# Seven block products in place of eight, and the order of the work behind two norms

## The reference

```
x = x + merged @ w_out                       # 512x1024 by 1024x1024
hn = rms_norm(x, ffn_norm)
up = causal_depthwise_conv(hn @ w_up, ffn_conv_w)
gate, val = split(up, 2)
x = x + (silu(gate) * val) @ w_down          # 512x2816 by 2816x1024
x = rms_norm(x, final_norm)
h = x @ w_in_2                               # first product of the second block
```

## Time and profile before

| what | us |
|---|---|
| runs | 1055.69, 1053.08, 1054.73 |
| median | 1054.73 |
| span of the profiled execution | 1050.5 |
| PE busy in it | 1038.4 |
| DVE, ACT, POOL busy | 593.9, 445.9, 51.0 |
| w_out, first matmul to the first transposes | 274.4 to 315.2 |
| norm 1 and `first_three` | 315.2 to 341.2 |
| first half of w_down begins | 444.7 |
| norm 2, first transposes | 681.0 |

### The profile page before, as it was taken

The page is one execution under the profiler, slowest core; times in us unless marked ns, Lnnn a source line. Parts: engine busy times, 40 slices in busy tenths (PEclk is TensorE's granted clock), DMA queues, the critical chain, the costliest instruction groups (busy, mean ns, idle before and its releaser), DMA issues.

```text
span 1050.5 us, 13952 instructions
## 1 busy us (share of the span) xinstructions
PE 1038.4 (99%) x5453; PEld 846.1 (81%) x5453; DVE 593.9 (57%) x1110; ACT 445.9 (42%) x855; POOL 51.0 (5%) x71
## 2 busy tenths in 40 slices
PE   9999999999999999999999999999999999999997
PEld 7877778888888888888888888899888677777785
DVE  6466665445356666533466563553456673567757
ACT  5355542233345434431234442453244454556640
POOL 0000000000001100000000000125200001000000
PEclk9999999999999999999999999999999999999999
DMA  7421133222341842333122323334211222511012
GB/s 277 160 65 57 61 101 100 95 89 98 123 140 41 275 152 87 98 125 110 61 101 85 100 97 110 131 122 135 91 61 61 61 81 71 211 41 41 21 61 80
DMA packets 29106, 107.08 MB, mean 102 GB/s; under 512 B 3227, under 2 KB 3371, under 8 KB 28401
## 3 DMA queue, kind: packets, MB, share of 16 engines
q1 hardware_dynamic: 24864, 86.13, 24.8%
q0 software_dynamic: 4032, 19.96, 5.3%
q10 hardware_dynamic: 144, 0.10, 0.0%
HBM read 101.44 MB, written 7.36 MB: 104 GB/s over the span
## 4 chain that ended last, share of the span: by engine, by line
PE 88%; DVE 5%; ACT 4%; issue 2%; DMA 2%; DVEq 0%; SPq 0%; ACTq 0%
PE ps L780 26%; PE ps L782 25%; PE ps L781 25%; PE ps L1054 2%; PE ps L1222 2%; PE ps L1205 1%; PE ps L1187 1%; DMA raw<-wp 1%; ACT whi L1285 1%; PE ps L1143 1%; PE ps L1106 1%; ACT SC L1336 1%; PE ps L1175 1%; DVE wlo L1633 0%; DVE SC L1739 0%
## 5 line engine op out<-in xcount | busy, mean ns | idle before, releaser
L780 PE MATMUL ps<-XH,whi 128*128 128x512 f32 (+1 forms) x864 | 336.7, 390 | 0.6 <-DVE XL L1646 0.2
L782 PE MATMUL ps<-XH,wlo 128*128 128x512 f32 (+1 forms) x864 | 326.9, 378 | 0.0
L781 PE MATMUL ps<-XL,whi 128*128 128x512 f32 (+1 forms) x864 | 326.5, 378 | 0.0
L1633 DVE TENSOR_TENSOR wlo<-raw,whi 128x1024 fp32r<-128x1024 f32 (+1 forms) x158 | 191.6, 1218 | 166.7 <-ACT whi L1285 166.1
L1285 ACT CAST whi<-raw 128x1024 fp32r<-128x1024 f32 (+1 forms) x158 | 161.2, 1027 | 95.9 <-PE ps L782 70.5
L780 PEld LDWEIGHTS ps<-XH,whi 128*128 128x128 f32 x864 | 162.6, 188 | 43.0 <-issue 12.4
L782 PEld LDWEIGHTS ps<-XH,wlo 128*128 128x128 f32 x864 | 162.6, 188 | 31.2
L781 PEld LDWEIGHTS ps<-XL,whi 128*128 128x128 f32 x864 | 162.8, 188 | 27.8 <-issue 0.5
L780 PE MATMUL ps<-whi,GH 128*128 128x512 f32 x176 | 68.8, 391 | 0.0
L782 PE MATMUL ps<-whi,GL 128*128 128x512 f32 x176 | 68.5, 389 | 0.0
L781 PE MATMUL ps<-wlo,GH 128*128 128x512 f32 x176 | 68.5, 389 | 0.0
(11 more groups left out here) (305 smaller groups left out, 1333.1 us busy)
## 6 DMA issues: line engine op xcount, KB each, us to landing
raw<-wp SPq DMA_DIRECT2D x150, 512.0 KB, 3.5
vec_dram<-row_dram POOLq DMA_DIRECT2D x1, 3072.0 KB, 13.7
H<-x POOLq DMA_DIRECT2D x1, 2048.0 KB, 8.1
x_dram<-H POOLq DMA_DIRECT2D x1, 2048.0 KB, 8.8
A<-w1c POOLq DMA_DIRECT2D x2, 1024.0 KB, 6.3
A<-x_dram POOLq DMA_DIRECT2D x1, 2048.0 KB, 12.8
y<-A SPq DMA_DIRECT2D x8, 256.0 KB, 2.0
raw<-wp SPq DMA_DIRECT2D x4, 402.0 KB, 3.9
```

Source lines behind the costliest of these rows:

```text
L780: self.e.matmul(o, ah, bh, start=start, stop=False)
L781: self.e.matmul(o, ah, bl, start=False, stop=False)
L782: return self.e.matmul(o, al, bh, start=False, stop=stop)
L1633: self.e.tensor_tensor(wlo[BUF[i]][:, 0:w], raw[i % NR][:, 0:w], whi[BUF[i]][:, 0:w].bitcast(F), ALU.subtract).then_inc(sems["lo"], 1)
```

## The change

**Seven products.** w_out and w_down are done in blocks of two by two (Winograd's form of Strassen's scheme): tokens in halves of 256, weight rows in alternate pieces, columns in halves of 512. There are four groups G: w_out (G = 0, 4 pairs of pieces) and w_down in three parts (G = 1, 2, 3 with 4, 4 and 3 pairs), each behind its own up tiles (`TILES_OF`: 8, 8, 6). A group is seven products p of two row tiles r; a product's r takes 12 matmuls (9 in G = 3), and the operands are MW or GW, seven blocks, with sums of left blocks among them. The matmuls are 168, 168, 168 and 126 where they were 192 and 528; results are added to or subtracted from `H` once per product and r, for p = 5 twice, 16 instructions a group.

**Sums of the left blocks** are made ahead, on DVE (`sums_of`, one 128x256 instruction for an even piece, three for an odd one), and split on ACT and DVE (`whole`, `summed`).

**Sums of the weights** (products 2, 3, 5 and 6) are made by DMAs that POOL issues with an add into `X0`/`Y0` or `X1`/`Y1`: 16 of 512 KB for each group, of which 10 add (`wino_sums`). Products 0, 1 and 4 still come through SP's ring. Each product needs two slots to be split, so a group has 14 splits; each slot now serves 12 matmuls instead of 24.

**Norms.** `rows_normed` gives way to `group_normed`: rows 0 and 1 are final after product 4, rows 2 and 3 after product 6. Their norms are placed inside products 5 and 6. In `first_three`, the transposes of row tile 2 stand behind the first halves of two tiles, those of tile 3 behind the third's. `biases` is called after f = 3 instead of after f = 10.

The core of the diff:

```diff
-    def rows_normed(m, rows):
-        for t in range(3):
-            rows(t)
-            if t == 2:
-                en.turn(m, 0)
-            en.norm_rest(m, t)
+    def product(G, p, between=None):
+        u = unit(G, p, 0)
+        en.split_all(u + 4)
+        en.wino(G, p, 0)
+        if between:
+            between(0)
+        en.split_all(u + 5)
+        en.wino(G, p, 1)
+        if between:
+            between(1)
+
+    def group(G, sums):
+        product(G, 0, sums)
+        product(G, 1)
+        en.wino_sums(G, 2)
+        product(G, 2)
+        en.wino_sums(G, 3)
+        product(G, 3)
+
+    def group_normed(G, m, sums):
+        group(G, sums)
+        product(G, 4)
+        en.eps_on(m, 0)
+        en.eps_on(m, 1)
+        u = unit(G, 6, 0)
+        en.split_all(u + 2)
+        en.wino(G, 5, 0)
+        en.norm_rest(m, 0)
+        en.norm_rest(m, 1)
+        en.wino(G, 5, 1)
+        en.eps_on(m, 2)
+        en.eps_on(m, 3)
+        en.split_all(u + 4)
+        en.wino(G, 6, 0)
+        en.turn(m, 0)
         en.turn(m, 1)
-        rows(3)
+        en.split_all(u + 5)
+        en.wino(G, 6, 1)
+        en.norm_rest(m, 2)
         en.norm_rest(m, 3)
-        en.turn(m, 2)
 
     def first_three(m, i, tile, tiles):
         en.part(i, 0, 0)
         en.part(i, 1, 0)
+        en.turn(m, 2)
+        en.part(i, 2, 0)
         en.turn(m, 3)
-        en.part(i, 2, 0)
         en.split_all(i + 4)
         for n in range(3):
             en.part(i, n, 1)
```

The products on PE, the adds on DVE, the squares and the weights' sums:

```diff
+            def wino(self, G, p, r):
+                t, n = WBANKS[p][r], OPERAND[p]
+                W = GW if G else MW
+                if p == 0:
+                    self.wait_ge("res", added(G - 1, 5, r))
+                    self.wait_ge("tt", 32)
+                    self.wait_ge("cp", 16)
+                elif p == 1:
+                    self.wait_ge("res", added(G - 1, 6, r))
+                elif p == 2:
+                    if G == 0:
+                        self.wait_ge("bm", 16)
+                        self.wait_ge("rsc", SCALED_GATE + 16)
+                    else:
+                        self.wait_ge("ub", 4 * (FIRST_F[G] + TILES_OF[G]))
+                        self.wait_ge("ve", 1)
+                    self.wait_ge("res", added(G - 1, 4, r))
+                else:
+                    self.wait_ge("res", added(G, {3: 0, 4: 2, 5: 3, 6: 1}[p], r))
+                at = 16 + 2 * FIRST_F[G] if G else 0
+                ts = slice(r * P, (r + 1) * P)
+                for s in range(2):
+                    i = unit(G, p, s)
+                    self.wait_ge("hi", i + 2)
+                    self.wait_ge("lo", i + 2)
+                    for m in range(2 * s, min(2 * s + 2, PAIRS[G])):
+                        self.wait_ge("gl", at + 4 * m + (1, 2, 3, 4, 4, 3, 2)[p])
+                        ws = slice((m % 2) * 512, (m % 2) * 512 + 512)
+                        f = self.mm3(ps[t][:, :], W[:, n, 0, m, ts], W[:, n, 1, m, ts], whi[BUF[i]][:, ws],
+                                     wlo[BUF[i]][:, ws], p in (0, 1, 2, 6) and m == 0, m == PAIRS[G] - 1, True)
+                    if r:
+                        f.then_inc(sems["used"], 1)
+                if r == 0:
+                    f.then_inc(sems["tm"], 1)
...
             def turn(self, m, t):
                 src = NORMED[m]
                 for c, ready in enumerate(("nlo", "nhi")):
                     self.wait_ge(ready, 4 * (m - 1) + t + 1)
                     if t == 3 and c:
-                        self.wait_ge("sq", sums_at(m, 2, 1))
+                        self.wait_ge("res", added(NORMED_BY[m], 6, 0))
                     elif t > 1:
                         self.wait_ge("xl", 8 * m + 2 * (t - 2) + c + 1)
                     else:
-                        self.wait_ge("sq", sums_at(m, 1, 1))
-                        self.wait_ge("tt", 32)
-                        if m == 2:
-                            self.wait_ge("ve", 1)
+                        self.wait_ge("res", added(NORMED_BY[m], 4 if t else 5, 1))
                     for k in range(4):
                         i = self.e.transpose(ps[NORM_BANKS[t][c]][:, k * P:(k + 1) * P],
                                              src[:, t, (4 * c + k) * P:(4 * c + k + 1) * P], ID)
...
+            def wino(self, G, p, r):
+                half, c = INTO[p]
+                h = H[:, 2 * half + r, c * 512:c * 512 + 512]
+                if r:
+                    self.wait_ge("used", unit(G, p, 1) + 1)
+                else:
+                    self.wait_ge("tm", 3 + 7 * G + p + 1)
+                self.wait_ge("xn", 16)
+                back, q = BEFORE[p]
+                self.wait_ge("res", added(G - back, q, r))
+                if p in (3, 5):
+                    self.e.tensor_tensor(h, h, ps[WBANKS[p][r]][:, :], ALU.subtract).then_inc(sems["res"], 1)
+                else:
+                    self.e.tensor_tensor(h, ps[WBANKS[p][r]][:, :], h, ALU.add).then_inc(sems["res"], 1)
+                if p == 5:
+                    h = H[:, 2 + r, 0:512]
+                    self.wait_ge("res", added(G - 1, 6, r))
+                    self.e.tensor_tensor(h, ps[WBANKS[p][r]][:, :], h, ALU.add).then_inc(sems["res"], 1)
 
...
+            def wino(self, G, p, r):
+                if G in (0, LAST_G) and p in (1, 4, 5, 6):
+                    half, c = INTO[p]
+                    self.wait_ge("res", added(G, p, r))
+                    if G == 0:
+                        self.wait_ge("gl", 16)
+                    else:
+                        self.wait_ge("gl", 60)
+                    self.square(2 if G else 1, 2 * half + r, c, p in (4, 6), (UA if G else GA)[:, 0, 0, :])
...
+            def sums_of(self, X, parity, at):
+                (a11, a21), (a12, a22) = ((X[:, i, 0, 0:256], X[:, i, 0, 256:512]) for i in range(2))
+                s3, s1 = X[:, 0, 1, 0:256], X[:, 0, 1, 256:512]
+                s2, s4 = X[:, 1, 1, 0:256], X[:, 1, 1, 256:512]
+                self.wait_ge("gl", at)
+                if parity == 0:
+                    self.e.tensor_tensor(s3, a11, a21, ALU.subtract).then_inc(sems["ms"], 1)
+                else:
+                    self.e.tensor_tensor(s1, a21, a22, ALU.subtract).then_inc(sems["ms"], 1)
+                    self.wait_ge("ms", at + 2)
+                    self.e.tensor_tensor(s2, s1, a11, ALU.subtract).then_inc(sems["ms"], 1)
+                    self.wait_ge("ms", at + 3)
...
+            def wino_sums(self, G, k):
+                if k == 0:
+                    if G:
+                        self.wait_ge("mc", N_MC)
+                    else:
+                        self.wait_ge("used", SLOT_GATE)
+                    for s in range(2):
+                        if G:
+                            self.wait_ge("lo", unit(G - 1, 6, s) + 2)
+                        self.add_x(G, B11, s, 1)
+                    for s in range(2):
+                        self.wait_ge(f"wx{s}", 64 * G + 16)
+                        self.add_x(G, B12, s, 2)
+                    for s in range(2):
+                        self.wait_ge(f"wx{s}", 64 * G + 32)
+                        self.add_x(G, B22, s, 3)
+                elif k == 1:
+                    if G == 0:
+                        self.wait_ge("used", SLOT_WOUT - 1)
+                    for s in range(2):
+                        if G:
+                            self.wait_ge("lo", unit(G - 1, 5, s) + 2)
+                        self.add_y(G, B11, s, 1)
+                    for s in range(2):
+                        self.wait_ge(f"wy{s}", 64 * G + 16)
+                        self.add_y(G, B12, s, 2)
+                elif k == 2:
+                    for s in range(2):
+                        self.wait_ge(f"wy{s}", 64 * G + 32)
+                        self.wait_ge("lo", unit(G, 2, s) + 2)
+                        self.add_y(G, B12, s, 1)
+                    for s in range(2):
+                        self.wait_ge(f"wy{s}", 64 * G + 48)
+                        self.add_y(G, B22, s, 2)
+                else:
+                    for s in range(2):
+                        self.wait_ge(f"wx{s}", 64 * G + 48)
+                        self.wait_ge("lo", unit(G, 3, s) + 2)
+                        self.add_x(G, B21, s, 4)
 
             def distances(self):
```

491 lines of the change are left out of this document (295 added, 196 removed).

## The result

The changed kernel takes **1061.5 us**, the median of 4 runs (1058.3 to 1062.3), where the kernel before takes 1053.9 (4 runs). The ratio is 1.0066, 95% interval 1.0048 to 1.0085: slower by 7.0 us by the ratio and 7.6 by medians, where 4.4 more, 1059.2, was predicted; it lies inside the range of 1049 to 1070. The profiled execution took 1061.4 us, with a span of 1059.6; that of before had a span of 1050.5.

A forecast was written before the change was run, and what follows sets the result against it. PE, busy 99% of the span, was taken to bound the kernel. 26.2 us of new waits, less 1.4 of old waits and 20.4 of removed work, made +4.4 us: 1054.7 becomes 1059.2, range 1049 to 1070.

The forecast's parts named there:

- The work removed: In the product stages, 90 fewer matmuls at 0.227 us each, all on the path: -20.4 us.
- Product 1: Waits for its slots' splits behind the last left piece: 0.5 (G = 0), 2.6 (G = 1 and 2), 3.5 us (G = 3).
- The norms: DVE and ACT chains outlast PE's work: waits 3.1, 3.9, 1.15 us in norm 1; 5.8, 4.5, 1.15 in norm 2.
- The second wait: Ahead of each norm's first half-width matmul, PE waits for `XL`: 3.9 us in norm 1, 4.5 in norm 2.
- rival B: Chains at the norms start late, only with product 5's second row tile: 10.5 us less, 1048.7; chance 0.13.
- The sum: Whole kernel: 26.2 us of waits come, 1.4 go, 20.4 of work go: +4.4 us.
- 4.2 us around the span: Time the runs hold outside the profiled span, taking a span of about 1055 to 1059.2 us.
- rival D: Clock falls in the new gaps; ahead of the halves it costs 3 to 6 us a norm, 1062 to 1070; chance 0.16.
- rival E: Adding DMAs of the weight sums are slow: 1064 us and more, some 32 us at the upper end; chance 0.11.
- C: Half way: waits 2 to 7 us shorter than counted, 1052 to 1057 us; chance 0.18.
- the signs: Unchanged matmul pitch, named waits at product 1 and norms; clock under 1.00 or ACT's DMA waits; wrong under 12 us at norms.
- A: The chains at product 1 and the norms as worked out: 1056 to 1062 us, likeliest 1059.2; chance 0.42.

The follow-up runs named there:

- experiment 2: Changed kernel with the splits of product 1's two slots ahead of the last up tile in G = 1, 2, 3: 1054.7 us.
- experiment 3: Changed kernel with 45 unread matmuls of 512 columns filling PE's three long waits, ahead of product 1 of G = 3 and both norms' first transposes: 1062.4 us.
- experiment 5: Changed kernel with DVE's and ACT's steps from product 4 to the norm's last split reordered, PE's order the same: 1047.2 us.
- kernel 7: Changed kernel with product 1's splits early, DVE's and ACT's steps at the norms reordered, and the fourth row tile's transposes early: 1039.9 us.
- kernels 8: kernel 7 with two ACT table loads moved up and product 1's squares moved behind the casts of product 3's slots: 1044.4 us.
- 10: kernel 7 with table loads and product 1's squares moved, and its adding DMAs as plain copies: 1039.2 us.
- 9: kernel 7 with its adding DMAs as plain copies, sums of right-hand blocks left out: 1037.5 us.
- 11: kernel 7 with only ACT's two table loads moved up, squares where they were: 1040.2 us.

## Why the prediction was right, point by point

**The work removed.** Right: the page counts 5363 matmuls instead of those of the earlier trace rows, 90 fewer, at the same pitch of 0.227 us.

**Product 1.** Predicted 0.5, 1.3, 1.3 and 3.5 us; by starts 0.59, 1.07, 1.07 and 3.58, and behind the last one 2.9 us of half-rate matmuls that the sum did not have. The chain behind the last left piece, with the table load in G = 3, was read right from the earlier trace rows, and experiment 2 took it away.

**The norms.** Predicted were 3.1 + 3.9 + 1.15 in norm 1 and 5.8 + 4.5 + 1.15 in norm 2. By starts there are 3.10 + 1.65 + 1.20 and 4.69 + 2.50 + 1.20, 14.3 us in all for 19.6. The places and the releasers are as named. The second wait looks less than half as long as foretold, but it is not the chain that was shorter: PE reached it later, since its transposes took 3.2 us each time instead of 1.67. With PE at full rate (experiment 3) the second wait was 3.2 and 4.0 us by starts, so the term was mis-sized by 0.7 and 0.5 us, and the first one of norm 2 by 1.1. These steps rest on an order that could have been otherwise, which experiment 5 shows. The prediction did not ask that, though its own count for rival B, 13.7 us of chain where under 8 would do, pointed at it.

**The sum.** 26.2 us of waits were predicted. Measured are 20.7 at the places named, 0.9 at product 3's second slot in w_out, which I had not seen (DVE's add, ACT's square, its cast and DVE's subtraction follow each other twice there, behind casts of `Y` that waited 1.1 and 0.9 us for their adds), and 6.3 of half-rate work (1.5 + 0.2 at each norm and 2.9 in G = 3). Together 27.9, less 20.4 and 1.4 makes +6.1, beside the +6.7 of the stages. By stage: w_out with norm 1 +2.6 for +1.8; G = 1 and G = 2 -4.0 and -4.4 for -4.1 each; G = 3 with norm 2 +12.3 for +10.9. That the number came out so near is in part luck: 5.5 us of waits too many were foretold, and 7.2 us of half-rate work and of the wait in product 3 were not. At the norms the two are one mechanism, since the slow transposes shortened the second waits; the 2.9 in G = 3 and the 0.9 are not.

One step of the sum was wrong without harm: the runs do not hold 4.2 us around the span, as the text on the kernel before has it too. The profiled execution took 1061.4 with a span of 1059.6, and in every run the difference is 1.6 to 1.9 us. The profiled execution of before, with 1050.5, was thus a fast one, near 1052.2, and not the median. The forecast is a difference added to the median, so it stands; but 9.1 us between the two profiles says 1.5 more than the medians do.

**The clock, rival D.** The clock fell in new gaps, but not where D had it: D put the fall in front of the halves, 3 to 6 us a norm, and there it kept 1.00; it fell in front of the transposes and of product 1 of G = 3. The rule of the Trainium skill (TensorE: Matmul & The Clock Gate, "HAM oscillation — how this bites in real kernels") would have made 1071. The granted clock agrees with the rule that the loss is paid anew behind each long wait. But the half-rate work stood ahead of another wait of the same chain, and most of the lost time was taken out of that. Where experiment 3 moved the fall in front of the halves, it did cost, 2.6 us in norm 1 and 1.5 in norm 2, less than D's 3 to 6. So D's fall is real, its price was somewhat high and its place was wrong, and the place decides.

**The adds, rival E.** I took a time near the copy's 3.6 us and no cost. They took 7.2 and 8.3 us in the median. The figure of the Trainium skill (Collectives: The Full Stack, "The bandwidth ceiling: the fold count and why AG ≠ RS ≠ AR"), as an estimate 1.93 times the copy's time, was 6.9 us; against the same lines as copies the measured factor is 1.4 to 1.5, but a copy in this traffic also takes 4.8 to 6.0 us and not 3.6, so the two errors nearly cancel. Their cost was 2.9 us by medians with overlapping intervals and 1.3 in the changed stages of the two traces. "No cost" was wrong by 2.9 us at most.

**The chances.** B and C, the cases under 1057, were not seen: the chain did not start late. Of the signs, the count and pitch of the matmuls, the releasers, 3.6 us ahead of product 1 of G = 3 and 3.1 at norm 1 came as written, and the waits at the norms were over 12 us, 14.3. The first wait of norm 2 was 4.7 where 5 to 6 was written, the second waits 1.65 and 2.5 where about 4 and 4 to 5 were. The signs of D and of E showed too (granted clock 0.50 in both norms; ACT waited 24.3 us in all for `Y`), in a kernel whose time is A's. They tell that a thing happened, not that it costs.

## What to carry to other kernels

Where PE waits for a row of steps that DVE and ACT do in a fixed order, write down when each step's input is ready and when its result is needed, and sort the steps by need before giving up work-saving: here three reorderings turned a loss of 7 us into a gain of 14, with not one instruction less. Low clock and waits on one chain are not to be added: first ask what PE would do with the time it gets back. If another wait of the chain follows, the slow work is free; if not, it costs in full. And once one bound is lifted, price the next (here the adding DMAs) anew, since its cost in the slower kernel says little of its cost in the faster one.

## What the hardware showed beside this

An adding DMA of 512 KB took 1.4 to 1.5 times as long to land as a copy on the same queue with the same waits. The granted clock fell to half at the end of waits of PE of 2.9, 3.4 and 4.5 us in the changed kernel, and kept 1.00 through its waits of 1.5 and 2.3 us ahead of the first half-width matmuls. It also fell with no wait of PE in front, at 24 matmuls of two columns or within 1.5 us behind them, in nine of the thirteen traces of the same instructions. In kernel 7 it also fell at 670, where waits of 1.46 and 1.03 us stand 2 us apart:

```profile
670.00:671.00 1.00, 0.56 (x3) 0.52 0.00 0
671.00:672.00 1.00, 1.00 (x7) 0.50 0.00 0
```

So two shorter waits close together went with what one long wait brought in the changed kernel. At the same place the clock also fell in kernels 8 (waits of 1.83 and 1.15 us) and 10 (1.63 and 1.03), and kept 1.00 in 9 and 11, where the first of the two was 0.52 and 0.53 and the second 1.03 as in kernel 7.
